# Output projection on high and low parts, two row buffers, and a reordered route stage in a streaming-encoder block

## The reference

```python
mod = silu(c) @ w_ada + b_ada            # six rows of 1024: sh1 sc1 gt1 sh2 sc2 gt2
h = rms_norm(x, g_mix_pre) * (1 + sc1) + sh1
...                                      # projections, conv; group A: mLSTM, 4 heads x 128 -> hm
...                                      # group B: indexer picks 128 keys, 4 heads x 128 -> ha
y = concatenate([hm, ha], -1) @ w_out    # 512x1024 @ 1024x1024
x = x + gt1 * rms_norm(y, g_mix_post)
h2 = rms_norm(x, g_ffn_pre) * (1 + sc2) + sh2
scores = sigmoid(h2 @ w_router)          # 64 experts in 8 groups, top 4 groups, top 8 experts
y2 = sum over chosen experts of gate * (silu(h2 @ wg) * (h2 @ wu)) @ wd   +  the shared expert
x = x + gt2 * rms_norm(y2, g_ffn_post)
```

## Time and profile before

| what | us |
|---|---|
| median of 3 runs (lowest, highest) | 1129.18 (1128.34, 1131.72) |
| the profiled execution, its time | 1132.51 |
| its span, first to last instruction | 1130.7 |
| sparse attention loop, about | 242 to 279.8 |
| route stage | 280.1 to 393.7 |
| experts | 394 to 1104 |
| final loop | 1104 to 1130.7 |

### The profile page before, as it was taken

How to read it: one execution, slowest core, us unless ns; L and a number is a source line. 1 busy time by engine, 2 the same in 40 slices (tenths; PEclk the granted TensorE clock), 3 DMA queues, 4 the chain that set the end, 5 groups by cost and what they waited for, 6 DMA issues and landing times.

```text
span 1130.7 us, 16022 instructions
## 1 busy us (share of the span) xinstructions
PE 1037.0 (92%) x4777; PEld 733.0 (65%) x4778; DVE 836.9 (74%) x1480; ACT 521.8 (46%) x610; POOL 234.5 (21%) x145
## 2 busy tenths in 40 slices
PE   1899997978998989999998999999999999899995
PEld 1898887657446447766775666667766666566662
DVE  4887899886665457787876787778787776676865
ACT  3425463364111145555554554555555454545542
POOL 0000000100000034353321323423222222342210
PEclk9899998989996999999999999999999999999998
DMA  9775300600948078999999999999999999999944
GB/s 358 244 277 178 101 1 1 229 14 13 388 186 327 27 249 269 356 344 343 338 366 348 323 333 344 345 337 329 324 338 333 346 308 339 304 328 334 340 113 152
DMA packets 82999, 297.60 MB, mean 263 GB/s; under 512 B 10799, under 2 KB 23131, under 8 KB 73437
## 3 DMA queue, kind: packets, MB, share of 16 engines
q1 hardware_dynamic: 69188, 259.12, 63.6%
q0 software_dynamic: 12208, 34.62, 13.4%
q10 hardware_dynamic: 1514, 2.97, 0.7%
HBM read 274.71 MB, written 24.12 MB: 264 GB/s over the span
## 4 chain that ended last, share of the span: by engine, by line
DMA 37%; PE 13%; issue 7%; POOLq 3%; DVE 3%; SPq 2%; ACT 1%; POOL 0%; DVEq 0%; ACTq 0%
DMA y_rows<-yb,row_numbers 28%; PE ps L2034 6%; DMA side<-in_w_exp_up 5%; PE ps L2089 4%; DMA main<-in_w_exp_up 2%; POOLq L1757 2%; DMA xg<-h_rows,row_numbers 1%; SPq L1573 1%; PE ps L2024 1%; PE ps L2134 1%; POOLq L1751 1%; ACT w_gate_up_hi L1802 1%; DVE main L2008 0%; DVE w_gate_up_lo L1901 0%; DVE pick L1881 0%
## 5 line engine op out<-in xcount | busy, mean ns | idle before, releaser
L1901 DVE TENSOR_TENSOR w_gate_up_lo<-side,w_gate_up_hi 128x2048 fp32r<-128x2048 f32 x64 | 146.8, 2294 | 78.9 <-ACT w_gate_up_hi L1802 78.8
L1901 DVE TENSOR_TENSOR w_gate_up_lo<-main,w_gate_up_hi 128x2048 fp32r<-128x2048 f32 x64 | 146.7, 2292 | 71.9 <-ACT w_gate_up_hi L1802 71.8
L1594 POOL DMA_INDIRECT y_rows<-yb,row_numbers x62 | 116.2, 1874 | 375.3 <-issue 311.4
L1802 ACT ACTIVATE w_gate_up_hi<-side 128x2048 fp32r<-128x2048 f32 x64 | 122.1, 1910 | 95.5 <-DMA side<-in_w_exp_up 54.1
L1802 ACT ACTIVATE w_gate_up_hi<-main 128x2048 fp32r<-128x2048 f32 x64 | 122.2, 1910 | 91.5 <-PE ps L2034 45.8
L2034 PE MATMUL ps<-w_gate_up_hi,xT_hi 128*128 128x512 f32 x512 | 144.7, 404 | 11.8 <-DVE xT_lo L1905 8.7
L2034 PE MATMUL ps<-w_gate_up_hi,xT_lo 128*128 128x512 f32 x512 | 137.6, 390 | 0.0
L2034 PE MATMUL ps<-w_gate_up_lo,xT_hi 128*128 128x512 f32 x512 | 137.3, 390 | 0.0
L2034 PEld LDWEIGHTS ps<-w_gate_up_hi,xT_hi 128*128 128x128 f32 x512 | 91.4, 189 | 32.1 <-issue 14.2
L2034 PEld LDWEIGHTS ps<-w_gate_up_hi,xT_lo 128*128 128x128 f32 x512 | 96.2, 188 | 21.1
L2034 PEld LDWEIGHTS ps<-w_gate_up_lo,xT_hi 128*128 128x128 f32 x512 | 96.1, 188 | 21.0
(11 more groups left out here) (309 smaller groups left out, 1554.9 us busy)
## 6 DMA issues: line engine op xcount, KB each, us to landing
side<-in_w_exp_gate SPq DMA_DIRECT2D x60, 512.0 KB, 9.6
side<-in_w_exp_up SPq DMA_DIRECT2D x60, 512.0 KB, 23.9
main<-in_w_exp_gate SPq DMA_DIRECT2D x60, 512.0 KB, 9.9
main<-in_w_exp_up SPq DMA_DIRECT2D x60, 512.0 KB, 24.6
side<-in_w_ada SPq DMA_DIRECT2D x20, 1024.0 KB, 7.7
main<-in_w_exp_down SPq DMA_DIRECT2D x16, 1024.0 KB, 23.1
maskb<-in_w_exp_down SPq DMA_DIRECT2D x16, 1024.0 KB, 20.4
side<-in_w_exp_down SPq DMA_DIRECT2D x16, 1024.0 KB, 23.6
```

The costliest lines, as they stand in the source:

```text
L1594: return pool.indirect_dma_start(out=G.y_sums, out_offset=bass.IndirectOffsetOnAxis(ap=sidx[0:rows, n:n + 1], axis=0), in_=yb[0:rows, slot ...
L1802: nc.scalar.activation(whi[:, half], wgu[n % RING][:, :, HALF * half:HALF * (half + 1), :] .rearrange("p m c f -> p c m f"), ACT.Copy).the ...
L1901: nc.vector.tensor_tensor(wlo[:, half], src, whi[:, half].bitcast(F32), ALU.subtract).then_inc(s_wlo, 1)
```

## The change

The output projection is done in three passes on fp32r parts: `catT` becomes `cat_hi` and `cat_lo`, `wout` gets `wout_hi` and `wout_lo`. In the sparse attention, ScalarE now writes the high part of each of the eight pieces and VectorE the low part. In the route stage ScalarE and VectorE split `wout` piece by piece ahead of a first projection tile that follows them. `h2n` has two buffers in the memory of `maskb` in place of four in that of `nat`; its stores have a semaphore for each tile. The pieces of modulation slice 4, quarters 0 and 1, are added in the attention loop, at u = 7, 9, 11 and 13. The route's lists are reordered: `turn` between half tiles, the shared expert's first two products done on 384 columns early and on the rest later, `shared(1, 0)` ahead of `places`, and the weight loads in another order (gate/up 2 and 3 and down 1 and 2 among them, whose memory now holds `wout_hi` or the row buffers until the projection and the transposes are done). The final loop adds the next tile's sums after the scaling.

```diff
@@ stage_attention, ScalarE
+            def high_head(h):
+                act.wait_ge(s_hT, h + 1)
+                nc.scalar.activation(cat_hi[:, h, :], ps[:, 7, :], ACT.Copy, scale=cols[:, 40 + h:41 + h]).then_inc(s_hTh, 1)
+            def high_out(h):
+                act.wait_ge(s_o, NT * (h + 1))
+                nc.scalar.activation(cat_hi[:, HEADS + h, :], ps[:, 6 + h % 2, :], ACT.Copy).then_inc(s_oh, 1)
...
                 if u:
                     copy_pT(u - 1)
+                if 2 <= u < HEADS + 2:
+                    high_head(u - 2)
+                if u >= NT + 2 and (u - 2) % NT == 0:
+                    high_out((u - 2) // NT - 1)
             copy_pT(len(UNITS) - 1)
+            high_out(HEADS - 1)
@@ stage_attention, VectorE
             def copy_out(h):
-                dve.wait_ge(s_o, NT * (h + 1))
-                nc.vector.tensor_copy(catT[:, HEADS + h, :], ps[:, 6 + h % 2, :]).then_inc(s_od, 1)
+                dve.wait_ge(s_oh, h + 1)
+                nc.vector.tensor_tensor(cat_lo[:, HEADS + h, :], ps[:, 6 + h % 2, :], cat_hi[:, HEADS + h, :].bitcast(F32),
+                                        ALU.subtract).then_inc(s_od, 1)
             def copy_head(h):
-                dve.wait_ge(s_hT, h + 1)
-                nc.vector.tensor_scalar(catT[:, h, :], ps[:, 7, :], cols[:, 40 + h:41 + h], None, ALU.mult).then_inc(s_hTd, 1)
+                dve.wait_ge(s_hTh, h + 1)
+                nc.vector.scalar_tensor_tensor(cat_lo[:, h, :], ps[:, 7, :], cols[:, 40 + h:41 + h], cat_hi[:, h, :].bitcast(F32),
+                                               ALU.mult, ALU.subtract).then_inc(s_hTd, 1)
+            def modulate(n):
...
+                if n < 4:
+                    step(nc.vector.scalar_tensor_tensor(rows[:, 2, :], G.row_pieces[n // 2][:, n % 2, :], G.cs[:, n:n + 1], rows[:, 2, :],
+                                                        ALU.mult, ALU.add))
...
+                if u >= 7 and u % 2:
+                    modulate((u - 7) // 2)
@@ stage_route
-        PIECES = [(s, q) for s in (4, 5) for q in range(4)]
+        PIECES = [(4, 2), (4, 3)] + [(5, q) for q in range(4)]
-        TURNED = [[], [], [0, 1], [2]]
+        TURNED = [[], [], [0], [1, 2]]
@@ SP
+            for n in (2, 3):
+                sp.wait_ge(s_used, n - 1)
+                load_piece(n)
+            store_h2(0)
+            store_h2(1)
             for n in (4, 5):
                 sp.wait_ge(s_used, n - 1)
                 load_piece(n)
-            load_gate_up(3)
-            load_down(1)
-            load_down(2)
...
             sp.wait_ge(s_y, NT)
...
             load_gate_up(0)
             load_gate_up(1)
-            sp.wait_ge(s_used, 8)
+            store_h2(2)
+            store_h2(3)
+            sp.dma_start(wd, A["w_sh_down"][0].rearrange("(f p) n -> p f n", p=P)).then_inc(s_wsd, 16)
+            sp.wait_ge(s_used, 6)
             load_down(0)
+            load_down(1)
+            load_gate_up(2)
+            load_gate_up(3)
...
             sp.wait_ge(s_h2T, 2 * NT)
-            load_gate_up(2)
+            load_down(2)
@@ ScalarE, at the start
+            act.wait_ge(G.s_wout, 16)
+            for f in range(2 * HEADS):
+                nc.scalar.activation(whi[:, f, :], wout[:, f, :], ACT.Copy).then_inc(s_whi, 1)
@@ VectorE
-            for n in range(4):
+            for f in range(2 * HEADS):
+                dve.wait_ge(s_whi, f + 1)
+                nc.vector.tensor_tensor(wlo[:, f, :], wout[:, f, :], whi[:, f, :].bitcast(F32), ALU.subtract).then_inc(s_wlo, 1)
+            for n in range(2):
                 modulate(n)
...
+                if i >= 2:
+                    dve.wait_ge(s_h2T, 2 * (i - 1))
+                    dve.wait_ge(s_hw[i - 2], 16)
...
-                for n in ((4, 5), (6,), (7,), ())[i]:
+                for n in ((), (2, 3), (), (4, 5))[i]:
                     modulate(n)
@@ TensorE
                     for f in range(2 * HEADS):
-                        ins = nc.tensor.matmul(ps[:, 2 * i + half, :], catT[:, f, i * P:(i + 1) * P],
-                                               wout[:, f, 512 * half:512 * (half + 1)], start=f == 0, stop=f == 2 * HEADS - 1)
+                        for j, (cp, wp) in enumerate(((cat_hi, whi), (cat_lo, whi), (cat_hi, wlo))):
+                            ins = nc.tensor.matmul(ps[:, 2 * i + half, :], cp[:, f, i * P:(i + 1) * P], wp[:, f, 512 * half:512 * (half + 1)],
+                                                   start=f == 0 and j == 0, stop=f == 2 * HEADS - 1 and j == 2)
+            def project_first():
+                for f in range(2 * HEADS):
+                    for j, (cp, wp) in enumerate(((cat_hi, whi), (cat_lo, whi), (cat_hi, wlo))):
+                        pe.wait_ge((s_whi, s_whi, s_wlo)[j], f + 1)
+                        for half in range(2):
+                            ins = nc.tensor.matmul(ps[:, half, :], cp[:, f, 0:P], wp[:, f, 512 * half:512 * (half + 1)],
+                                                   start=f == 0 and j == 0, stop=f == 2 * HEADS - 1 and j == 2)
...
-            pe.wait_ge(G.s_wout, 16)
-            project_out(0)
+            project_first()
             project_out(1, [0])
-            pe.wait_ge(s_used, 4)
+            pe.wait_ge(s_used, 2)
             sum_rows(0, 2)
             project_out(1, [1])
-            project_out(2)
+            project_out(2, [0])
             turn(0)
+            project_out(2, [1])
+            pe.wait_ge(s_rowd, 2)
+            project_out(3, [0])
             turn(1)
-            pe.wait_ge(s_rowd, 2)
-            project_out(3)
+            project_out(3, [1])
+            pe.wait_ge(s_in, 32)
             turn(2)
             pe.wait_ge(s_h2Td, 2 * (NT - 1))
...
+            pe.wait_ge(s_wsh, 32)
+            shared(0, 0, 0, (NT - 1) * P)
             turn(NT - 1)
+            shared(0, 1, 0, (NT - 1) * P)
             pe.wait_ge(s_h2Td, 2 * NT)
             router(NT - 1)
-            pe.wait_ge(s_wsh, 48)
-            shared(0, 0)
-            shared(0, 1)
+            shared(0, 0, (NT - 1) * P, SEQ)
+            shared(0, 1, (NT - 1) * P, SEQ)
+            shared(1, 0)
             places()
-            pe.wait_ge(s_used, 8)
+            pe.wait_ge(s_used, 6)
             sum_rows(2, 4)
-            shared(1, 0)
@@ stage_experts, final loop on VectorE
                 for i in range(NT):
-                    if i + 1 < NT:
-                        add_sums(i + 1)
...
-                    last(nc.vector.scalar_tensor_tensor(y[:, i, :], y[:, i, :], rt[:, i:i + 1], G.rows[:, 3, :], ALU.mult, ALU.mult))
+                    nc.vector.scalar_tensor_tensor(y[:, i, :], y[:, i, :], rt[:, i:i + 1], G.rows[:, 3, :], ALU.mult, ALU.mult).then_inc(s_y, 1)
+                    if i + 1 < NT:
+                        add_sums(i + 1)
+                    dve.wait_ge(s_y, i + 1)
                     nc.vector.tensor_tensor(xt[:, i, :], xt[:, i, :], y[:, i, :], ALU.add).then_inc(s_o[i], 1)
```

79 lines of the change are left out of this document (43 added, 36 removed).

## The result

| kernel | median us (lowest, highest; runs) | ratio to before (95%) |
|---|---|---|
| before | 1129.35 (1128.34, 1131.72; 4) | |
| changed | 1142.78 (1139.59, 1147.07; 4) | 1.0122 (1.0097, 1.0146) |
| changed, a second set | 1140.97 (1137.94, 1144.22; 4), before 1129.12 in it | 1.0117 (1.0099, 1.0135) |

The account below looks back on a forecast made before the run. Experts take most time at DMA share 0.99, unchanged; attention is a relay, TensorE the route's path. Attention +7.6, projection -9.6, behind it +3.3, final loop -0.7, clock +3.7 make +4.3: 1133.5 us, range 1126.5 to 1138.5.

Parts of the forecast that it names:

- the paragraph on the clock: TensorE's clock falls to 0.50 behind three new route pauses, costing 3.7 us, from 6.4 if paid in full.
- The joints: Sparse attention at u = 6, 10, 14: VectorE's mask delayed behind ScalarE's high part, 1.6 to 2.0 us each, 5.6 in all.
- the sign: Sign of being right: three VectorE waits of 2 us or more at the low-part subtraction, released by ScalarE.
- The upper bound of 10 for the attention: Attention stage: +10 us instead of +7.6 if every modulate is on the path.
- The projection: Route: 192 fp32r products at 0.229 us replace 64 fp32 ones, VectorE in time; -9.6 us up to turn(2).
- one sign of being wrong: Route: logits more than 2 us from 78 us after the route's start.
- Behind the projection: Route from turn(2) to the last shared product: 57.0 us against 53.8, called +3.3, with waits before routers and diagonals.
- The final loop: End of the kernel: scaling goes ahead of the next tile's sums, -0.7 us.
- Late weights: Rival, chance 0.10: SP's new load order makes early experts wait, +8 to +15 us, 1138 to 1145.
- The clock stays up: Rival, chance 0.32: same work without new clock falls, +0.6 us, 1129.8, range 1128 to 1132.
- The joints are absorbed: Rival, chance 0.13: attention waits vanish, projection's gain survives, 1124 to 1128; attention stage less than 3 us longer.

Follow-up runs that it names:

- e4: Changed kernel with two unused products on TensorE ahead of its wait in units 6, 10 and 14: 1138.86 us, ratio 1.0061.
- e1: Changed kernel with VectorE's low part of each head's output made one round later: 1131.5 us, ratio 1.0028.
- e5: Changed kernel with ScalarE making the high part ahead of its copy of the turned probabilities: 1132.34 us, ratio 1.0030.
- e2: Kernel before, with ScalarE copying heads 0 to 2 first and VectorE waiting for that and copying again: 1137.88 us, ratio 1.0082.
- e12: Changed kernel with the low part one round later and half the last shared product ahead of the diagonals' wait: 1125.86 us, ratio 0.9961.
- e14: Changed kernel with low part one round later, half the last shared product ahead of the diagonals, tile 1's copy early, four unused route products: 1117.85 us.
- e6: Changed kernel with columns 0 to 255 of the last shared product run ahead of the diagonals' wait: 1133.47 us, ratio 1.0034.
- e15: Changed kernel with the first store of the shared expert's rows issued later, behind ScalarE's second copy: 1140.41 us, ratio 1.0083.
- e7: Changed kernel with VectorE's copy of tile 1's transposes back in its old, earlier place: 1137.81 us, ratio 1.0067.
- e10: Changed kernel with six unused products, two ahead of the projection and four ahead of the routers: 1134.04 us, ratio 1.0038.
- e11: Changed kernel with low part one round later, half the last shared product ahead of the diagonals, tile 1's copy early: 1121.74 us, ratio 0.9945.

## Why the prediction was wrong

**The step that failed is the paragraph on the clock**, "I take 1.0 + 1.0 + 0.5 + 1.2 = 3.7". It listed three pauses, all in the route, and none in the attention loop, though the same text made TensorE's pause at each joint 2 us longer: the loop's clock stood at nothing in the sum, without a reason. The runs showed falls to 0.50 for about 3 us behind these pauses, behind all three in the first profile and behind two in the second. By e4, which keeps the waits and takes the falls away, three cost 3.7 us and two 1.9. e1 and e5 take the wait and with it the fall, and shorten the loop by 4.9 to 7.7 us. The 1.05 us pause ahead of the route, which cost nothing, was no guide to pauses of 1.9 to 2.7.

**The joints** were right as a mechanism and nearly in size: three waits of VectorE on ScalarE's high part, 0.74, 2.06 and 2.06 us (the sign asked for three of 2 us or more; the first is less). A joint alone costs 1.9 at full clock (e2), and joints and modulates together 7.5 (e4) against 7.0. TensorE's extra idle time in the loop, 5.0 and 5.2 us, is smaller, and its extra busy time, 6.2 and 3.6, is larger than the falls' price of 3.7 and 1.9: where the clock is low its products fill time that it would have stood. Neither is a price by itself; the runs with the one and without the other give it. The upper bound of 10 for the attention doesn't follow from its terms: with all four modulates on the path they add up to 11.3.

**The projection**: 0.229 us a product was right, six half tiles of 5.5 were right, VectorE was in time. The first product came 1.1 us behind the stage's start, as said. With the clock at full, from it to turn(2) takes 48.6 (e12, e14) and not 47.8, and with the fall 50.1 and 51.0: this clock price is 1.5 to 2.4, not 1.0. Together that is the 1.3 to 2.2 us by which the projection gained less than -8.6. So one sign of being wrong came: the logits were ready 82.0 and 82.9 us behind the route's start, where 78 and at most 2 more were named.

**Behind the projection** every step came within 0.5 us: 5.64 against 5.7, the diagonals 50.8 behind turn(2) against 51.0, the end 59.9 against 59.7 (the +3.3 is 57.0 - 53.8 = 3.2, a slip of 0.1). The sum of it is better than its reasons: it took the routers' 9.00 us for their full-speed price and a low clock for 1.6 on top, and e14 shows 5.57. Most of the clock's price there was already in the kernel before, and 9.00 held it. The gain of doing the shared products early did go to the diagonals' wait, and e6 got it back.

**The final loop** was right (-0.8 against -0.7). **Late weights** did not come: no product of the first experts waited for them. **The clock stays up** fell, with 0.50 at every pause forecast and at two or three more. **The joints are absorbed** fell by the waits themselves, by e1 and e2, and by an attention stage 8.8 and 11.2 us longer, where it asked for less than 3.

**What stays open.** The stages from the loop to the experts and the final loop give +9.8 and +8.3 us in the two profiles, 5.5 and 4.0 above the forecast: 4.2 and 1.8 in the attention, 1.3 and 2.2 in the projection. The medians give +13.4 and +11.9, and the other 3.6 us are not located. The prediction let the profile of the kernel before stand 3.3 above its median and carried that over; the two profiles of the changed kernel stand 4.3 above and 3.0 below theirs, so such a difference doesn't carry over. A candidate is the experts, 703.9 to 714.1 us long over the 14 profiles in which their code is the same. The change leaves their code alone but not how they start. In the six profiles where the clock fell on their first products, both of the kernel before's code among them, they took 706.7 on the mean (703.9 to 710.4) and their third load of gate weights was issued 25.8 to 27.0 us behind their start. In the eight where it did not, both of the changed kernel among them, it was 709.9 (707.5 to 714.1) and 29.6 to 31.8. The size fits, but this compares profiles and is no experiment; e15 accounts for part of it at most. Counted from the second set, e4, e7 and e10 gained just what their offsets say, e12 and e14 under 2 us more, and e1, e5, e6 and e11 some 4 us more. No run separates this.

The Trainium skill (TensorE: Matmul & The Clock Gate, Part 1) says that throttled is the default and that sustained activity releases it. The trace agrees in the routers, where it was 0.50 before and after and 1.00 in e10 and e14, which fill their pause. Behind the joints it agrees in part: 0.50 behind three, two and one of three (first profile, second, e2). In the first projection tile it was 0.50 in both profiles, and 1.00 in e12, which leaves that pause of 2.76 us as it is. At the experts' start of the changed kernel it stayed at 1.00 behind a pause of 1.98 us, as the last section shows. It was weighed for the route alone; applied to the loop as well it would have given the missing term its sign.

## What to carry over

When a change lengthens a wait in a relay between engines, list every pause that TensorE then has, price the wait, and price the products behind it at the low clock too, as a range that starts at nothing: here a joint cost 1.9 us as a wait and another 1.0 to 1.5 where the clock fell behind it. A value that one engine derives from another's result should be taken a round later than it could be, or be made ahead of the other engine's next wait. Work that has no dependence on a wait (half of a product's columns) belongs ahead of it, and a pause that can't be filled with work was cheaper here when filled with unused products, in the loop (e4) and ahead of the routers (e10); ahead of the projection they gained nothing.

Don't read a price off idle or busy time alone. At a low clock busy time grows and idle time shrinks with the same work; compare runs that have the wait and not the fall, and the other way round.
